# Odd mixer: per-token scalars spread by one f32r matmul from masked rows, forgetting attention in two one-bank chains among the projections

## The reference, cut to what matters

```python
def forgetting_attention(q, k, v, log_f):
    c = jnp.cumsum(log_f, axis=1)
    ...
        s = jnp.einsum('bhqd,bkhd->bhqk', q_i, k).astype(jnp.float32) * scale
        s = s + c_i[..., None] - ck[:, :, None, :]
        s = jnp.where(_block_mask(i, S), s, -jnp.inf)
        p = jax.nn.softmax(s, axis=-1)
        return jnp.einsum('bhqk,bkhd->bqhd', p.astype(v.dtype), v)
...
def gated_delta_rule(q, k, v, g, beta):
    ...
    a_mat = jnp.where(strict, jnp.einsum('bhncd,bhned->bhnce', k_beta, k) * decay, 0.0)
    t_inv = lax.linalg.triangular_solve(eye + a_mat, ...)
    ...
        v_new = u_i - jnp.einsum('bhcd,bhde->bhce', w_i, state)
        o_i = (jnp.einsum('bhcd,bhde->bhce', q_i * jnp.exp(g_i)[..., None], state)
               + jnp.einsum('bhce,bhed->bhcd', qk_i, v_new))
        state = (state * jnp.exp(g_last)[..., None]
                 + jnp.einsum('bhcd,bhce->bhde', k_i * jnp.exp(g_last - g_i)[..., None], v_new))
```

## Time and profile before

| | us |
|---|---|
| median of 3 runs | 1397.97 |
| lowest, highest | 1394.88, 1398.94 |
| the profiled execution, whole | 1395.86 |
| its span, first to last instruction | 1394.1 |
| PE busy | 1344.4 (96%) |
| DVE busy | 640.8 (46%) |
| ACT busy | 502.9 (36%) |
| mean granted clock of PE | 0.984 |

### The profile page before, as it was taken

The page is one execution under the profiler, slowest core; times in us unless marked ns, Lnnn a source line. Parts: engine busy times, 40 slices in busy tenths (PEclk is TensorE's granted clock), DMA queues, the critical chain, the costliest instruction groups (busy, mean ns, idle before and its releaser), DMA issues.

```text
span 1394.1 us, 17352 instructions
## 1 busy us (share of the span) xinstructions
PE 1344.4 (96%) x6558; PEld 1076.0 (77%) x6558; DVE 640.8 (46%) x903; ACT 502.9 (36%) x723; POOL 14.9 (1%) x22
## 2 busy tenths in 40 slices
PE   9999999999999999999989999787999999999997
PEld 6766457888888878888878888666888888887886
DVE  6665533644444432247654336452554444443224
ACT  6344333433333321135652333443433333331111
POOL 0000000000000000000010100000000000000000
PEclk9999999999999999999999999899999999999998
DMA  6222210232222322222211111000232223222221
GB/s 241 91 91 78 88 38 27 95 117 94 90 90 100 109 92 92 102 78 91 81 65 51 50 42 61 31 0 1 76 105 91 90 90 105 105 90 103 93 75 61
DMA packets 34081, 114.10 MB, mean 82 GB/s; under 512 B 4466, under 2 KB 4722, under 8 KB 34034
## 3 DMA queue, kind: packets, MB, share of 16 engines
q1 hardware_dynamic: 34034, 113.43, 23.6%
HBM read 106.89 MB, written 2.10 MB: 78 GB/s over the span
## 4 chain that ended last, share of the span: by engine, by line
PE 91%; DVE 4%; ACT 3%; issue 1%; SPq 1%; DMA 0%; DVEq 0%; ACTq 0%
PE PS L1339 89%; PE PS L1415 1%; PE PS L1748 1%; DVE hbuf L1184 1%; SPq L493 1%; ACT wring L572 0%; DVE outT L1333 0%; DVE wring L949 0%; ACT L787 0%; DVE G L1248 0%; DVE fbuf L1282 0%; DMA xT<-x_t 0%; DVE tbuf L1274 0%; DVE qT L1312 0%; DVE amax L1276 0%
## 5 line engine op out<-in xcount | busy, mean ns | idle before, releaser
L1339 PE MATMUL PS<-HH,wring 128*128 128x512 f32 x3096 | 732.1, 394 | 0.0
L1339 PEld LDWEIGHTS PS<-HH,wring 128*128 128x128 f32 x3096 | 576.6, 188 | 121.2 <-issue 4.4
L1339 PE MATMUL PS<-AA,wring 128*128 (+1 forms) x1344 | 319.6, 398 | 5.0 <-issue 1.8
L1339 PEld LDWEIGHTS PS<-AA,wring 128*128 128x128 f32 x1344 | 253.0, 189 | 67.5 <-issue 2.7
L920 DVE TENSOR_TENSOR ubuf<-PS,rstd 128x512 f32<-128x512 f32 x44 | 30.4, 691 | 198.1 <-PE PS L1339 198.1
L942 DVE TENSOR_TENSOR wring<-raw,wring 128x1024 fp32r<-128x1024 f32 x36 | 44.1, 1226 | 155.2 <-ACT wring L623 155.2
L929 DVE TENSOR_TENSOR wring<-raw,wring 128x1024 fp32r<-128x1024 f32 x88 | 107.5, 1222 | 1.0 <-ACT wring L615 0.4
L949 DVE TENSOR_TENSOR wring<-raw,wring 128x1024 fp32r<-128x1024 f32 x70 | 85.8, 1228 | 47.5 <-ACT wring L572 47.5
L610 ACT ACTIVATE AA<-ubuf 128x512 f32 x44 | 27.9, 635 | 198.4 <-DVE ubuf L927 198.4
L572 ACT ACTIVATE wring<-raw 128x1024 fp32r<-128x1024 f32 x70 | 73.5, 1054 | 68.5 <-PE PS L1339 50.9
L623 ACT ACTIVATE wring<-raw 128x1024 fp32r<-128x1024 f32 x36 | 38.2, 1062 | 161.1 <-PE PS L1339 161.1
(11 more groups left out here) (243 smaller groups left out, 1027.4 us busy)
## 6 DMA issues: line engine op xcount, KB each, us to landing
raw<-w_stream SPq DMA_DIRECT2D x194, 512.0 KB, 3.2
reps<-ub SPq DMA_DIRECT2D x64, 67.5 KB, 2.0
out_t<-outT SPq DMA_DIRECT2D x8, 256.0 KB, 2.2
xT<-x_t SPq DMA_DIRECT2D x3, 512.0 KB, 8.3
first_raw<-w_stream SPq DMA_DIRECT2D x2, 512.0 KB, 9.5
rope<-rope_const SPq DMA_DIRECT2D x1, 576.0 KB, 6.8
consts<-shape_const SPq DMA_DIRECT2D x1, 576.0 KB, 7.6
xT<-x_t SPq DMA_DIRECT2D x2, 256.0 KB, 3.7
```

The costliest lines, as they stand in the source:

```text
L1339: return nc.tensor.matmul(out, lhsT, rhs, start=start, stop=stop)
```

## The change

- **Scalars.** One tensor `scal` holds total, cumulative and forget sums, kscal and qscal. `delta_scalars` (moved from projection 11 to 10, with the l2 sums moved from 10 to 9) splits 64 columns of it in a high and a low part (`pairs`); PE transposes them once, and DVE multiplies the transposed rows by a mask into `rows` (128 partitions by 512 columns, f32r). A broadcast column of `pick` against `rows` (`picked`) then gives the spread scalars of four heads in one 512-column f32r matmul.
- **Forget sums.** `fox_s` adds them on PE with one more f32r matmul; `cb`, `tbuf` and the subtraction on DVE go, and the maximum and the exponential read PSUM.
- **Attention.** Units of even and odd number are two chains, each with one bank (0 or 1) for scores, transposes and values in turn. Buffers moved out of `HH`'s place, so units may stand among the projections. Values are projected first (12 to 15), then q and k of each head (16 to 23), then z, all but the values in banks 2 and 3.
- **Order.** A string of letters, `PLAN`, says from which of eight streams the next item comes.
- **Places in memory.** `at_A`, where `AA` and all behind it starts, is now rounded so that its offset leaves the same remainder in 256 bytes as `at_H`. By the program's sums it was 129,024 (remainder 0) and is 129,152 (remainder 128); `wring` and `HH` start at 41,088 and 73,856 (both 128) in both.
- **Even mixer.** `ln_bc` stands two items earlier; the output projection takes k = 4, 5 for all four banks and then k = 6, 7 bank by bank.

The diff, cut to its core:

```diff
-    at_A = p = (p + 2848 + 127) // 128 * 128
+    at_A = p = (p + 2848 - at_H % 256 + 255) // 256 * 256 + at_H % 256
...
+            if e == 11:
+                pe.wait_ge(sem("pairs_ready"), 1)
+                both = pairs[:].rearrange("p a b -> p (a b)").bitcast(f32)
+                nc.tensor.transpose(PS[:, ROWS_BANK, 0:P], both, ident).then_inc(sem("pairs_t"), 1)
+        def picked(out, n, columns=S, start=True, stop=True):
+            every = rows[:].rearrange("p a b -> p (a b)")
+            return mm(out, pick[:, n:n + 1].to_broadcast([P, P]), every[:, 0:columns], start, stop)
...
-                for h in range(H):
-                    spread(PS[:, X, blk(h)], gcum[:, 0, i, h:h + 1])
-                    last = spread(PS[:, Y, blk(h)], kscal[:, 0, i, h:h + 1])
+                picked(PS[:, X], PICK_CUM + i)
+                last = picked(PS[:, Y], PICK_K + i)
...
             mm(PS[:, u % 2, 0:n], qd[:, h, blk(i)], kd[:, h, 0:n], True, False)
+            picked(PS[:, u % 2, 0:n], PICK_FORGET + h, n, False, False)
...
-            link(V.scalar_tensor_tensor(tbuf[:, u % 2, 0:n], cb[:, h, 0:n], gcum[:, 2, i, h:h + 1], PS[:, u % 2, 0:n],
-                                        ALU.subtract, ALU.subtract))
-            V.tensor_reduce(amax[:, 0, u % 2:u % 2 + 1], tbuf[:, u % 2, 0:n], AX.X, ALU.min).then_inc(sem("fox_min"), 1)
+            V.tensor_reduce(amax[:, 0, u % 2:u % 2 + 1], PS[:, u % 2, 0:(u % NB + 1) * P], AX.X, ALU.max, negate=True).then_inc(sem("fox_max"), 1)
...
+        def fox_values(u):
+            h, i = UNITS[u]
+            pe.wait_ge(sem("fox_wt"), u + 1)
+            for j in range(i + 1):
+                last = mm(PS[:, u % 2, 0:P], vd[:, j, blk(h)], FT[:, u % 2, j], j == 0, j == i)
+            last.then_inc(sem("fox_pv"), 1)
...
-        for k in range(4, KD):
+        for n, k in [(n, k) for k in (4, 5) for n in range(RING)] + [(n, k) for n in range(RING) for k in (6, 7)]:
...
+PLAN = ("tktttktatbttattttbtatbtttatabtatbabatabtabtabtatbtabtabtabtatbeeooabeotbeeaoeoebooeeaobeoateebtoaeae"
```

More of the change, by code:

```diff
@@ L153, in even_order @@
     return order + [("conv_lo", 3)]
[L156 to L170, removed]
@@ L173, in pe_cost @@
[L173 to L186, removed]
-def odd_order():
[L191 to L224, removed]
@@ new lines, in odd_streams, with fox @@
+def odd_streams():
+    def fox(n):
+        return [(kind, u) for u in range(n, H * NB, 2) for kind in ("fox_s", "fox_m", "fox_p", "fox_t", "fox_w", "fox_v", "fox_y")]
+    tiles = []
+    for e in range(12, 28):
+        tiles += [("tile", (e, part)) for part in range(4)] + [("evac", e)]
+        if e >= 24:
+            tiles.append(("z_silu", e - 24))
+    partial = [("out1", (n, k)) for n in range(RING) for k in range(H)]
+    gated = [item for a in range(NB) for item in (("gy", a), ("gy_lo", a))]
+    return {"a": gdn_steps(0), "b": gdn_steps(1), "e": fox(0), "o": fox(1), "t": tiles, "k": [("tok", 6), ("tok", 7)], "p": partial, "y": gated}
@@ L226 @@
+def odd_order():
+    streams = {name: iter(items) for name, items in odd_streams().items()}
+    order = [next(streams[name]) for name in PLAN]
+    assert all(not list(left) for left in streams.values())
+    return order
 LAMBDA_INIT = 0.8 - 0.6 * math.exp(-0.3 * 0)
@@ L355, in build @@
     at_z = q
+    fbuf, _ = at("fbuf", [2, S], f32, at_z)
+    FT, _ = at("FT", [2, NB, P], f32, at_z + 2 * S * 4)
     zT, q = at("zT", [H, S], f32, q)
+    last_fox, _ = at("last_fox", [2, S], f32r, q)
     qd, q = at("qd", [H, S], f32, q)
@@ L362, in build @@
     hrow, _ = at("hrow", [S], f32, at_z)
+    rows, q = at("rows", [H, P], f32r, at_A + 3 * 2 * S * 4)
+    pairs, q = at("pairs", [2, 4 * NB * H], f32r, q)
+    pick, q = at("pick", [16], f32r, q)
+    assert q <= at_A + 4 * 2 * S * 4
     q = at_A + 4 * 2 * S * 4
@@ L397, in hd, with fox_out @@
         return PS[:, ps_bank].rearrange("p (h c) -> p h c", h=H)
+    def fox_out(h, m):
+        return AA[:, h, m] if h < H - 1 else last_fox[:, m]
     def vcol(n):
@@ L1818, in _ @@
                 tok_transpose(a)
-            elif kind == "fox_cb":
-                if a == 0:
-                    pe.wait_ge(evacuated, E_OUT1)
-                if a >= 2:
-                    pe.wait_ge(sem("fox_y"), a - 1)
-                for b in range(NB):
-                    last = spread(PS[:, FOX_V, blk(b)], gcum[:, 2, b, a:a + 1])
-                last.then_inc(sem("fox_cb_mm"), 1)
             elif kind == "fox_s":
```

194 lines of the change are left out of this document (103 added, 91 removed).

## The result

The changed kernel takes **1342.09 us** (median of 4 runs, 1339.96 to 1343.14) beside 1397.32 (1394.88 to 1398.94) for the kernel before on the same chip: a ratio of 0.9604, interval 0.9584 to 0.9624. That is 55 us faster. The experiments ran in other sessions, in which the kernel before took 1396.32 to 1397.57 us, so a difference of 1 us from after says nothing.

What follows compares the result with a forecast made beforehand. PE was taken to bound the kernel, busy 1344.4 of 1394.1 us, so only less PE work or fewer stops help. Terms -3.3 - 8.7 - 7.4 - 15.9 - 4.6 = -39.9 gave 1358 us by the median, range 1347 to 1380.

Steps and rivals of the forecast that it cites:

- Even mixer, -3.3: Even mixer: PE's stops of 1.6 us for `AA` and 1.8 before the fifth bank both go, -3.3 us.
- Places in memory, -8.7: FFNs and output projections: 1440 matmuls reading `AA` or y get 0.006 us cheaper at remainder 128, -8.7 us.
- worth nothing: Rival on the place in memory: `AA` stays at 0.234 us a matmul, total 1367 us; chance 0.22.
- Scalars, -7.4: Odd mixer: spreads gone, -14.1 us; picked matmuls +2.9, forget sums +2.8, other +1.0; net -7.4, at worst -1.4.
- The +1.0 for changes between f32 and f32r: Part of the scalars' sum: transpose of `pairs` and more switches between f32 and f32r on PE, +1.0 us.
- The floor that I named for the picks: Sixteen forget matmuls in `fox_s`: no 128-column piece under 0.11 us (a weight load is 107 ns), taken as +2.8 us.
- Stops of PE, 27.9 to 12: Odd mixer: PE's idle stops fall from 27.9 us to 12, -15.9 us.
- fourth point: Remaining stops at handoffs of recurrence and attention: 24 instead of 6 under 1.5 us of cover; 9 us, ends 2 and 22.
- my four points: New stops in the odd mixer: `pairs` +1.7 us, values' tile 16 +0.3, end of `gy` +1.0, remaining handoffs 9; together 12.
- The tail that I put at 1.0: End of the odd mixer: four `gy` runs, some 13 us, covered by 11.5 + 0.9; a stop of +1.0 us.
- 4.6 for the clock: Odd mixer: PE's low clock level behind the long stop and from 952 goes, 2.3 us each, -4.6 us.
- The rival that attention brings its stops along: Odd mixer: queues of DVE and ACT keep 28 us of stops and the lower clock, +20.5, 1379 us; chance 0.12.

Runs made afterwards that it cites:

- the two medians: `at_A` rounded to remainder 128 as the only edit in the kernel before, 1387.55 us; `at_A` put back at remainder 0 in the kernel after, 1349.17 us.
- a_spreads: Kernel after, with steps 0 and 1 of the recurrence spread by 48 f32 matmuls of 128 columns instead of 12 picked ones: 1348.43 us.
- a_stops: Kernel after, with PE waiting at 20 places in the second FFN's gate and up projections until the tile just finished is emptied: stretch 22.4 us longer, median 20.
- a_stops_long: Kernel after, with PE waiting at 20 places of the second FFN until the gated activation's low part is written: 1439.18 us.
- the four orders of attention: Kernel after, with 33 or 22 of 33 projection items ahead of attention: rest spread evenly, 1381.68 and 1382.74 us; placed at the handoffs, 1367.41 and 1365.18.

## Why the prediction was too cautious, point by point

- *Even mixer, -3.3.* Right: -3.0 measured alone.
- *Places in memory, -8.7.* Right: 9.9 and 7.1 us by the two medians. By the stages it is 8.0 (2 x 3.44, 0.9 in the output projection, 0.2 in the stretch), and an estimate for the even mixer's output projection, which no stage shows alone, is 192 x 0.0066 = 1.3 more. The rival "worth nothing" is refuted, and with it the formula of the Trainium skill ("TensorE: Matmul & The Clock Gate", section "Back-to-back issue gap") that I had set against the term: it goes by the columns alone, and here the same 512 columns take 0.2267 or 0.2333 us. What I couldn't name is now narrower: same remainder, not remainder 128.
- *Scalars, -7.4.* Right: 7.6 for the recurrence's steps (`a_spreads`), 3.5 for the 32 pieces of `fox_cb` by their price of 0.11, less 2.6 for the forget picks, together -8.5. The +1.0 for changes between f32 and f32r wasn't seen. The floor that I named for the picks gives 4 x (0.11 + 0.12 + 0.17 + 0.23) = 2.5 and not the 2.8 that I took.
- *Stops of PE, 27.9 to 12.* **This is the step that failed**, and its fourth point in it: "I take 9 us". The list of waits has 2.8 where my four points gave 12. `pairs` came as forecast (1.6 for 1.7; it is ready at 711.7 where all comes 5.2 us sooner than in before, which is 716.9 for 716.7). The tail that I put at 1.0 does not stop: the last `y_low` ends 0.3 us ahead of the first `y_high` product. Of the 80 handoffs of the recurrence and 48 of attention two stop, for 1.2 us in all. I had counted how many had less than 1.5 us of cover, 24, and borrowed 5.7 us from today's window. But a handoff needs 1.0 to 1.1, and only six were under that; the 5.7 were long stops in particular places (2.5 at L1230, 1.3 at L1223 of before) that the new list doesn't have. The low end of 2 us that I gave was near what came, 1.2. I had also counted ten projections (58 us) as spread through attention; up to its last matmul there are 27 quarters (some 37 us), and the rest stands behind it.
- *What a stop costs.* The second error, of method: I priced a stop by its idle time and added 4.6 for the clock. The runs say more. In `a_stops` 15.7 us of idle cost 22.4, in `a_stops_long` 66.9 cost 100.9, in the four orders of attention 14.8 to 27.6 more idle than after cost 22.8 to 40.1: 1.4 to 1.7 us for each one shown. The stretch of before, less 8.5 for scalars and 0.2 for the place, is 35.7 longer than that of after for 25.1 of idle, so 10.6 don't show as idle. By the granted clock PE was busy at the lower level for 17.9 us of it (3.4 from 694.6, 3.4 from 732.1, 5.2 from 897.6, 5.9 from 950.6), and for 3.4 in after; half of the difference is 7.2. I had seen the last two of these places alone, and took 4.6. What is left, 3.4 over the 19 stops that went, is 0.2 a stop. In the four orders the same working leaves 0.2 to 0.4. The 0.33 was measured between matmuls of 512 columns only, while most stops of the mixer stand between small ones.

The sum: 3.0 + 8.0 + 1.3 + 8.5 + 35.7 = 56.5 us beside 55.2 measured, which is as near as medians and single profiles allow. Against my 39.9, 9.2 are stops that I expected and that didn't come, 6.0 the price of those that went (10.6 instead of 4.6), and the rest the small excesses of place and scalars. The rival that attention brings its stops along is refuted for this PLAN, but it was no idle one: four other orders of the same items cost 23 to 40 us in the stretch, more than the 20.5 that I gave it.

## What to carry to other kernels

Price a stop of PE as its idle time and 0.2 to 0.4 us more, and look up the granted clock behind it, since half of PE's time at the lower level is lost; many short stops are dearer than the list of waits says. For cover, ask of each handoff what stands between its two ends in PE's order; the amount of independent work in the neighbourhood decides nothing if it stands behind the waiting item. And give operands that PE reads together the same remainder in 256 bytes by a rule, which costs one line: here a table that grew by 20 columns would have changed it under the old rule.

## What the runs showed of the hardware

- An f32r matmul of 512 columns takes 0.2267 us where stationary and moving operand start at the same remainder of 256 bytes (both 128 or both 0) and 0.2333 where they differ by 128 (stationary at 128, moving at 0). Other differences weren't tried.
- Behind a stop, at a granted clock of 1.00, the second matmul starts 0.34 us after the first instead of 0.227, and the next four 0.23 to 0.24, whether the stop was 0.8 or 3.3 us.
- Stops of 0.8 us in every 12 left the granted clock at 1.00 over 264 us; stops of 3.3 in every 14 to 17 brought it to 0.90.
- A change of function between exponential and silu on ACT costs 1.28 us each way, with 0.01 to 0.02 us around it.
